# Two low halves by negative and added transfer, one folded sum of squares, and a late scaling of a third unit in a two-layer decoder trunk

## The chip, the cores and the metric

One Trainium2 chip, one core. The metric is the device time of one execution in microseconds, the median of repeated runs. All inputs and outputs are float32.

## The reference

`x` has 256 positions of 1024 channels, and two layers run one after the other.

```python
def pool_conv_layer(x, ...):                       # layer 0
    proj = rms_norm(x, norm_g) @ w_in
    a, bv, bg, z = split(proj)                     # 1024, 1024, 1024, 2048 channels
    ya = (multiscale_pool(a) @ pool_w per group) * pool_scale
    u = causal_depthwise_conv(bv * sigmoid(bg), width 31) + conv_b
    yb = silu(layer_norm(u))
    return (concat(ya, yb) * silu(z)) @ w_out      # added to x

def moba_layer(x, ...):                            # layer 1
    q, k, v, z = split(rms_norm(x, norm_g) @ w_in)
    q, k = rms_norm(q), rms_norm(k)                # by heads of 64 channels
    o = causal_attention(q, k, v) with ALiBi
    return (o * silu(z)) @ w_out                   # added to x
```

## The kernel before, in words

The weights are cut into 49 units of 128 partitions x 2048 columns (1 MB). A unit is one strip of 256 output channels, or 256 rows of an output projection. Names of units (lines 40 to 54): BG and BV (0 to 7), A (8 to 11), ZB (12 to 15), PW (16, the pooling maps), ZA (17 to 20, the gate of ya), OA (21 to 24, the output projection of ya), OB (25 to 28, that of yb), Z1 (29 to 32, layer 1's gate), six pairs of units for k, q and v (33 to 44), O1 (45 to 48).

Most products are made of three matmuls in a faster number format, `product` at line 1074: a float32 operand is split in a high half, rounded by a copy, and a low half, the rest. TensorE takes high x high, high x low and low x high. Five units (`NATIVE`) are multiplied in plain float32 instead; such a matmul appears as two records of the trace.

Each unit comes by a DMA of SyncE into one of four raw slots (L399); the load of unit n waits until unit n - 4 is no longer read. ScalarE copies each half of the unit to its high half (`cut_hi`, L461), which also waits for a free slot of high halves. For the low half there are two ways. VectorE subtracts, `cut_lo`, L740. Or, for the units of `ADDED` (10, 21, 22, 24), ScalarE writes the high half's negative (L464), and a transfer that POOL issues (`added_low`, L426) adds the raw half to it in memory; TensorE then waits for that transfer (`arrived`, line 1081).

The same split is made of the activations. For the output projection of ya, four pairs of tiles are multiplied by their gate on VectorE (L906), copied to `ya_hi` by ScalarE (`high_ya`, L519) and subtracted to `ya_lo` by VectorE (`low_ya`, L887). The pairs belong to units 21 to 24; unit 23 is native and needs no halves. The first two are subtracted after the taps of step 19, and units 21 and 22 wait for them at line 1209.

Every engine's order is written out by hand, step by step (`for n in range(1, OA[0] + 1)` at line 531 for ScalarE, at line 890 for VectorE). A planner (`conv_plan`, line 193) spreads the 31 taps of the depthwise convolution over the steps: some are single operations on VectorE (L856), some are two products on ScalarE (L548) and one addition of two tiles on VectorE (L860), and 28 of them are summed by transfers that POOL issues (L435), joined at L853. The planner counts a unit as 5.75 us (line 202), a native one as 6.9. When the taps are done, VectorE folds the channels' sum (`fold_mean`, L873), TensorE makes the mean of it in the midst of unit 23 (`channel_mean`, L1200), VectorE centres (L880), ScalarE squares (L469), VectorE folds (`fold`, L767), and TensorE makes the variance in the midst of unit 24 (`SUM2_AT`, L1154).

Layer 1 begins while layer 0's residual is still being added: VectorE adds pair by pair (L961), ScalarE squares (L469) and copies the high halves of the unnormalised h to `ya_hi` (L487), VectorE subtracts (`low_h`, L753). Units 29 and 30 (`EARLY`, line 243) are multiplied with these unnormalised halves. The norm's factor comes later: the squares are summed over channels by four matmuls of `square_sums` (L1154, lines 1257 to 1260), ScalarE takes the root (L473), VectorE the reciprocal (L773), and both units' results are multiplied by it out of PSUM on VectorE (`scale_late`, L793) and gated by ScalarE in place (`late_gate`, L492). Units 31 and 32 take the normalised h (`over_rms`, line 781), and ScalarE gates them out of PSUM itself (L675).

The end of that stage is ordered so. ScalarE: late gate 29, late gate 30, cut 33, gate 31, cut 34, gate 32 (lines 667 to 676). VectorE: late scaling 29, late scaling 30, low halves of 33, low halves of 34 (lines 1028 to 1032). From unit 33 on TensorE takes units in pairs, with the activations as stationary operand and 256 columns of each of the two units as one moving operand of 512 (`token_step`, line 1117): its first step waits for the first half of both.

## Time and profile before

| | us |
|---|---|
| median of 3 runs | 329.39 (329.38 to 329.5) |
| the profiled execution, its own time | 329.37 |
| its span, first to last instruction | 327.4 |
| TensorE busy | 321.8 (98%) |
| VectorE busy | 261.1 (80%) |
| ScalarE busy | 235.8 (72%) |
| GpSimd busy | 51.2 (16%) |

Mean granted clock of TensorE: 0.999 of full speed. Engines in rows: PE is TensorE's matmuls, DVE VectorE, ACT ScalarE, POOL GpSimd, SPq the queue of SyncE. L12 is line 12 of the kernel. In a timeline row the first number is the start in us from the start of the span, the second the time from the first start to the last end of the instructions that are merged in the row (their count stands behind x); a bracket gives the idle time of the engine ahead of it, and whose end it waited for. Instructions that follow each other on one engine overlap by about a tenth of a microsecond, so a row of four of 0.69 lasts less than 2.76.

### The profile page before, as it was taken

What the parts mean: (1) busy time and instruction counts of PE and PEld (TensorE: products, weight loads), DVE (VectorE), ACT (ScalarE), POOL (GpSimd) and SP (SyncE); (2) the same over time, 40 slices, a digit from 0 to 9 for tenths busy, and PEclk for the clock granted to TensorE, in tenths of its full rate; (3) what the DMA queues carried; (4) which work ended last, traced back from release to release, by engine and by line L of the source; (5) the groups of instructions that cost most, each with busy time, mean ns of one, the idle gap of its engine ahead of it and who ended that gap; (6) DMA issues with size and microseconds to landing.
All of it is one profiled execution on the core that took longest, in us unless ns stands there. A gap on an engine that the chain in (4) does not pass through costs nothing.

```text
span 327.4 us, 5849 instructions
## 1 busy us (share of the span) xinstructions
PE 321.8 (98%) x2244; PEld 295.5 (90%) x2244; DVE 261.1 (80%) x482; ACT 235.8 (72%) x436; POOL 51.2 (16%) x58
## 2 busy tenths in 40 slices
PE   8999999999999999998999999999999999999995
PEld 8899999999999999997999999988887777778885
DVE  2799989999999999999895898846556887758533
ACT  4687999997999889987766557814756667566630
POOL 0050024423224112120000000005500231400000
PEclk9999999999999999999999999999999999999999
DMA  7988478969999699984539244780635323200003
GB/s 275 413 278 355 156 265 224 203 148 344 346 328 214 122 411 292 217 270 93 249 143 397 104 148 152 279 322 13 243 130 166 132 103 129 114 2 0 2 0 130
DMA packets 12843, 64.79 MB, mean 198 GB/s; under 512 B 1424, under 2 KB 1552, under 8 KB 6544
## 3 DMA queue, kind: packets, MB, share of 16 engines
q1 hardware_dynamic: 8064, 53.78, 43.3%
q0 software_dynamic: 4608, 10.49, 17.7%
q8 instruction: 18, 0.29, 0.4%
q10 hardware_dynamic: 144, 0.15, 0.2%
q14 instruction: 9, 0.07, 0.1%
HBM read 52.88 MB, written 1.05 MB: 165 GB/s over the span
## 4 chain that ended last, share of the span: by engine, by line
PE 90%; ACT 4%; DVE 3%; issue 1%; POOL 0%; DVEq 0%; ACTq 0%; POOLq 0%
PE bank L1077 24%; PE bank L1078 23%; PE bank L1079 23%; PE bank L1111 4%; PE bank L1137 3%; PE bank L1185 2%; PE bank L1291 2%; PE bank L1318 2%; PE bank L1154 2%; PE bank L1145 2%; PE bank L1304 2%; ACT scratch L548 1%; DVE scratch L856 1%; ACT w_hi L461 1%; PE bank L1270 1%
## 5 line engine op out<-in xcount | busy, mean ns | idle before, releaser
L740 DVE TENSOR_TENSOR w_lo<-raw,w_hi 128x1024 fp32r<-128x1024 f32 x80 | 95.3, 1222 | 16.9 <-ACT w_hi L461 16.7
L461 ACT CAST w_hi<-raw 128x1024 fp32r<-128x1024 f32 x88 | 88.6, 1047 | 7.5 <-DMA raw<-w 3.8
L1077 PE MATMUL bank<-h_hi,w_hi 128*128 128x256 f32 x320 | 91.1, 285 | 0.0
L1079 PE MATMUL bank<-h_hi,w_lo 128*128 128x256 f32 x320 | 90.5, 283 | 0.0
L1078 PE MATMUL bank<-h_lo,w_hi 128*128 128x256 f32 x320 | 90.5, 283 | 0.0
L1078 PEld LDWEIGHTS bank<-h_lo,w_hi 128*128 128x128 f32 x320 | 61.4, 192 | 0.1
L1077 PEld LDWEIGHTS bank<-h_hi,w_hi 128*128 128x128 f32 x320 | 61.4, 192 | 0.1
L1079 PEld LDWEIGHTS bank<-h_hi,w_lo 128*128 128x128 f32 x320 | 61.4, 192 | 0.0
L856 DVE SCALAR_TENSOR_TENSOR scratch<-scratch,params 128x256 f32<-128x256 f32 x106 | 43.4, 482 | 0.2
L1077 PE MATMUL bank<-ya_hi,w_hi 128*128 128x256 f32 x144 | 42.6, 296 | 0.0
L1078 PE MATMUL bank<-ya_lo,w_hi 128*128 128x256 f32 x144 | 40.7, 282 | 0.0
L1079 PE MATMUL bank<-ya_hi,w_lo 128*128 128x256 f32 x144 | 40.7, 282 | 0.0
L1077 PE MATMUL bank<-w_hi,h_hi 128*128 128x512 f32 x96 | 39.2, 408 | 0.0
L1078 PE MATMUL bank<-w_lo,h_hi 128*128 128x512 f32 x96 | 37.6, 391 | 0.0
L1079 PE MATMUL bank<-w_hi,h_lo 128*128 128x512 f32 x96 | 37.5, 391 | 0.0
L548 ACT ACTIVATE scratch<-scratch,params 128x256 f32<-128x256 f32 x78 | 32.8, 504 | 0.0
L435 POOL DMA_DIRECT2D side_v<-side_ring x24 | 21.0, 905 | 73.9 <-ACT side_ring L528 52.8
L1077 PEld LDWEIGHTS bank<-ya_hi,w_hi 128*128 128x128 f32 x144 | 27.5, 191 | 2.0 <-issue 1.7
L1078 PEld LDWEIGHTS bank<-ya_lo,w_hi 128*128 128x128 f32 x144 | 27.5, 191 | 0.1
L1079 PEld LDWEIGHTS bank<-ya_hi,w_lo 128*128 128x128 f32 x144 | 27.5, 191 | 0.0
L860 DVE TENSOR_TENSOR scratch<-scratch 128x512 f32<-128x512 f32 x39 | 26.1, 690 | 1.0
L446 POOL TENSOR_SCALAR scratch<-scratch 128x8 f32<-128x8 f32 x8 | 5.1, 632 | 116.5 <-DVE scratch L1037 116.2
(106 smaller groups left out, 522.2 us busy)
## 6 DMA issues: line engine op xcount, KB each, us to landing
raw<-w SPq DMA_DIRECT2D x49, 1024.0 KB, 6.9
side_v<-side_ring POOLq DMA_DIRECT2D x24, 256.0 KB, 6.5
w_lo<-raw POOLq DMA_DIRECT2D x8, 512.0 KB, 7.3
X<-xT SPq DMA_DIRECT2D x2, 512.0 KB, 5.2
out<-X SPq DMA_DIRECT2D x4, 256.0 KB, 2.6
consts<-const SPq DMA_DIRECT2D x1, 290.0 KB, 13.3
params<-vec ACTq DMA_DIRECT2D x1, 149.0 KB, 4.9
```

The source lines that it names most:

```text
L435: pool.dma_start(side_v[:, pair, item % 2, :, :], side_home(pair, item), accum_op=ALU.add).then_inc(side_added[pair][item % 2], 16)
L461: nc.scalar.copy(halves(w_hi, cut_slot(n), half), halves(raw, n % RAW, half)).then_inc(hi_cut, 1)
L548: last = nc.scalar.mul(product_home(product)[:, i, :], U[:, c, k:k + S], column(CW + TAPS * c + k))
L740: nc.vector.tensor_tensor(halves(w_lo, cut_slot(n), half), halves(raw, n % RAW, half), halves(w_hi, cut_slot(n), half).bitcast(F32), ALU.s ...
L856: nc.vector.scalar_tensor_tensor(V[:, c, :], U[:, c, k:k + S], column(CW + TAPS * c + k), V[:, c, :], ALU.mult, ALU.add).then_inc(tap, 1)
L860: nc.vector.tensor_tensor(V[:, c:c + 2, :], V[:, c:c + 2, :], product_home(product), ALU.add).then_inc(tap, 1)
L1077: nc.tensor.matmul(dst, wh, ah, start=start, stop=False, skip_group_check=True)
L1078: nc.tensor.matmul(dst, wh, al, start=False, stop=False, skip_group_check=True)
L1079: return nc.tensor.matmul(dst, wl, ah, start=False, stop=stop, skip_group_check=True)
L1111: last = nc.tensor.matmul(dst, wr, (H if n else H0)[:, k, :], start=start, stop=stop, skip_group_check=True)
L1137: return nc.tensor.matmul(dst, wr, SZ[:, (KD if n in OB else 0) + tile, :], start=start and m % 2 == 0, stop=stop, skip_group_check=True)
L1145: nc.tensor.matmul(bank[7][:, 0:P], ones[:, :], ones[:, :], start=True, stop=True, skip_group_check=True)
```

## The change

Three parts. (A) The low halves of the first two gated pairs of ya are made as `ADDED` units are: after its copy ScalarE writes the negative into `ya_lo`, and a transfer of 256 KB that POOL issues adds the gated tiles. POOL's list is written out, with these two transfers between those of units 21 and 22; the copy and the negative of the second pair stand between the two halves of unit 22 on ScalarE; TensorE waits for the two transfers at units 21 and 22. VectorE's two subtractions are gone. (B) Layer 1's squares are folded on VectorE to one tile, by two more operations at step m = 4, and one matmul behind the sixth step of unit 29 takes the place of four matmuls behind its second and third. (C) Unit 31 joins the units that are multiplied with the unnormalised halves; VectorE scales it and ScalarE gates it in place. Unit 32 is then the first to wait for the normalised halves.

```diff
--- before.py
+++ after.py
@@ -123,6 +123,8 @@
     return sum(1 for n in units[:i] if n not in NATIVE)
 
 
+
+SQUARE_FOLDS = (0, 2, 2, 2), (0, 4, 2, 3), (0, 6, 2, 4), (0, 1, 1, 4)
 
 STEPS = 48
 CUT_HI_AT, CUT_LO_AT = (1, 7, 9, 15), (2, 8, 11, 15)
@@ -239,8 +241,9 @@
 
 
 MEAN_AT = 2, 0, 5
+SUM3_AT = 5
 SUM2_AT = 3, 0, 2
-EARLY = (BG[0],), (Z1[0], Z1[1])
+EARLY = (BG[0],), (Z1[0], Z1[1], Z1[2])
 
 
 def hybrid_trunk(nc, xT, w, vec, const, out):
@@ -331,7 +334,8 @@
         raw_in = [sem(f"raw_in{i}") for i in range(RAW)]
         ones_set, pads_set, qs_set = sem("ones_set"), sem("pads_set"), sem("qs_set")
         hi_cut, lo_cut = sem("hi_cut"), sem("lo_cut")
-        minus_hi = sem("minus_hi")
+        minus_hi, minus_ya = sem("minus_hi"), sem("minus_ya")
+        ya_added = [sem(f"ya_added{i}") for i in range(2)]
         lo_added = [[sem(f"lo_added{n}{half}") for half in range(2)] for n in ADDED]
         unit_done = sem("unit_done")
         sq_ready, folded = sem("sq_ready"), sem("folded")
@@ -418,10 +422,10 @@
                                     ALU.mult).then_inc(qs_set, 1)
             pool.wait_ge(pads_set, 3)
 
-            def added_low(n):
+            def added_low(n, parts=(0, 1)):
 
                 i = ADDED.index(n)
-                for half in range(2):
+                for half in parts:
                     pool.wait_ge(minus_hi, 2 * i + half + 1)
                     pool.dma_start(halves(w_lo, cut_slot(n), half).bitcast(F32), halves(raw, n % RAW, half),
                                    accum_op=ALU.add).then_inc(lo_added[i][half], 16)
@@ -437,9 +441,20 @@
                 if n + 3 in EARLY_ADDED:
                     added_low(n + 3)
 
-            for n in ADDED:
-                if n not in EARLY_ADDED:
-                    added_low(n)
+            def added_ya(i):
+
+                pool.wait_ge(minus_ya, i + 1)
+                pool.dma_start(ya_lo[:, 2 * i:2 * i + 2, :].bitcast(F32), SZ[:, 2 * i:2 * i + 2, :],
+                               accum_op=ALU.add).then_inc(ya_added[i], 16)
+
+            added_low(OA[0], (0,))
+            added_ya(0)
+            added_low(OA[0], (1,))
+            added_low(OA[1], (0,))
+            added_ya(1)
+            added_low(OA[1], (1,))
+            added_low(OA[3])
+
 
             for r in range(8):
                 pool.wait_ge(qk_ss, r + 1)
@@ -517,6 +532,10 @@
                 act.wait_ge(ya_ready, i + 1)
                 act.wait_ge(tap, max(FOLDED[2 * (i // 2):2 * (i // 2) + 2]))
                 nc.scalar.copy(ya_hi[:, 2 * i:2 * i + 2, :], SZ[:, 2 * i:2 * i + 2, :]).then_inc(yahi_ready, 1)
+                if i < 2:
+                    act.wait_ge(yahi_ready, i + 1)
+                    nc.scalar.mul(ya_lo[:, 2 * i:2 * i + 2, :], ya_hi[:, 2 * i:2 * i + 2, :].bitcast(F32),
+                                  -1.0).then_inc(minus_ya, 1)
 
             def side_product(pair, item):
 
@@ -535,8 +554,6 @@
                     cut_hi(OA[3], (0,))
                 if n == ZA[0]:
                     act.wait_ge(tap, PRODUCT_USED[LATE_FROM - 1])
-                if n == OA[0] - 2:
-                    high_ya(1)
                 for tiles, k, product, _, _ in CONV_PLAN.get(n, ()):
                     if product is None or k is None:
                         continue
@@ -549,7 +566,10 @@
                                              column(CW + TAPS * c + k))
                     last.then_inc(product_ready, 1)
                 if n + 3 in (OA[0], SPARE):
-                    cut_hi(n + 3, (0,) if n == ZA[1] else (0, 1))
+                    cut_hi(n + 3, (0,))
+                if n + 3 == SPARE:
+                    high_ya(1)
+                    cut_hi(SPARE, (1,))
                 if n == OA[0]:
                     cut_hi(OA[3], (1,))
                     high_ya(3)
@@ -755,14 +775,12 @@
 
             folds = 0
 
-            def fold(group, pairs):
+            def fold(group, first, last):
 
                 nonlocal folds
-                steps = ((0, 2, 2), (0, 4, 2), (0, 6, 2), (0, 1, 1)) if pairs == 4 else ((0, 2, 2), (0, 4, 2))
-                for i, (a, b, n) in enumerate(steps):
-                    if i < 3:
-                        dve.wait_ge(sq_ready, 4 * group + i + 2)
-                    if i:
+                for a, b, n, squares in SQUARE_FOLDS[first:last]:
+                    dve.wait_ge(sq_ready, 4 * group + squares)
+                    if first or (a, b) != SQUARE_FOLDS[first][:2]:
                         dve.wait_ge(folded, folds)
                     nc.vector.tensor_tensor(SQ[:, a:a + n, :], SQ[:, a:a + n, :], SQ[:, b:b + n, :],
                                             ALU.add).then_inc(folded, 1)
@@ -910,11 +928,11 @@
                     cut_lo(n + 2)
                 if n == OA[0]:
                     fold_mean()
-                for i in {ZA[2]: (0, 1), OA[0]: (3,)}.get(n, ()):
-                    low_ya(i)
+                if n == OA[0]:
+                    low_ya(3)
 
             centre()
-            fold(1, 4)
+            fold(1, 0, 4)
             cut_lo(OB[1], (0,))
             take_inverse(2)
             dve.wait_ge(sq_ready, 8)
@@ -967,10 +985,12 @@
                     residual(m, 0)
                     dve.wait_ge(x_updated, m + 1)
                     gained(1, m)
+                if m == 4:
+                    fold(2, 2, 4)
                 if m:
                     low_h(1, m - 1)
                 if m == 2:
-                    fold(2, 3)
+                    fold(2, 0, 2)
             cut_lo(Z1[1])
             take_inverse(3)
             cut_lo(Z1[2])
@@ -1206,7 +1226,7 @@
                 if n in NATIVE:
                     pe.wait_ge(ya_ready, i + 1)
                 else:
-                    pe.wait_ge(yalo_ready, pairs_cut(OA, i + 1))
+                    pe.wait_ge(*((ya_added[i], 16) if i < 2 else (yalo_ready, 1)))
                 for kt in range(2):
                     arrived(n, kt)
                     for m in range(KD):
@@ -1253,11 +1273,9 @@
                 if n % 4 == 0:
                     pe.wait_ge(root_ready, 3)
                 for k in range(KD):
-                    channel_step(n, k, {Z1[0]: 1, Z1[2]: 2}.get(n))
-                    if n == Z1[0] and k == 1:
-                        square_sums(6, (0, 1), bank[0], False)
-                    if n == Z1[0] and k == 2:
-                        square_sums(0, (6, 7), bank[0], True)
+                    channel_step(n, k, {Z1[0]: 1, Z1[3]: 2}.get(n))
+                    if n == Z1[0] and k == SUM3_AT:
+                        square_sums(8, (0,), bank[0], True)
 
             def turn_qk(octet, isq, half):
 
```

## Rows read from the trace of the kernel before

**Rows 1.** The page's first part: busy time, share of the span, instructions
```profile
PE 321.8 (98%) x2244; PEld 295.5 (90%) x2244; DVE 261.1 (80%) x482; ACT 235.8 (72%) x436; POOL 51.2 (16%) x58
```

**Rows 2.** The waits of TensorE: who for whom, us, times, longest
```profile
PE bank L1200 <- DVE scratch L873: 0.8, 1, 0.8
```

**Rows 3.** Timeline of TensorE: the start, and the two sums of layer 0
```profile
0.98 5.36 PE L1145 MATMUL bank<-ones 128*128 128x128 f32 x24 [0.98 <-POOL eps L411]
...
145.60 2.75 PE L1137 MATMUL bank<-scratch,raw 128*128 128x256 f32 x12
149.21 0.67 PE L1200 MATMUL bank<-scratch,ones 128*128 128x256 f32 x2 [0.84 <-DVE scratch L873]
...
155.10 0.70 PE L1154 MATMUL bank<-scratch,ones 128*128 128x256 f32 x2
```

**Rows 4.** Timeline of VectorE, 118 to 160 us
```profile
131.96 1.29 DVE L887 TENSOR_TENSOR ya_lo<-scratch,ya_hi 128x512 fp32r<-128x512 f32 x2
...
133.96 4.69 DVE L860 TENSOR_TENSOR scratch<-scratch 128x512 f32<-128x512 f32 x6
...
146.65 2.41 DVE L873 TENSOR_TENSOR scratch<-scratch 128x1024 f32<-128x1024 f32 x3 [0.23 <-DVE scratch L860]
...
152.31 2.74 DVE L767 TENSOR_TENSOR scratch<-scratch 128x512 f32<-128x512 f32 x4
```

**Rows 5.** Timeline of ScalarE, 118 to 160 us
```profile
122.82 1.05 ACT L461 CAST w_hi<-raw 128x1024 fp32r<-128x1024 f32 x1 [1.10 <-PE bank L1079]
123.90 1.07 ACT L464 ACTIVATE w_lo<-w_hi 128x1024 fp32r<-128x1024 f32 x1
...
125.35 0.61 ACT L519 CAST ya_hi<-scratch 128x512 fp32r<-128x512 f32 x1
...
132.96 4.90 ACT L548 ACTIVATE scratch<-scratch,params 128x256 f32<-128x256 f32 x12
...
148.74 1.99 ACT L461 CAST w_hi<-raw 128x1024 fp32r<-128x1024 f32 x2 [2.63 <-issue]
150.64 2.42 ACT L469 ACTIVATE scratch<-scratch 128x512 f32<-128x512 f32 x4
```

**Rows 6.** Timelines of GpSimd and of SyncE's queue: two issues
```profile
125.26 0.86 POOL L426 DMA_DIRECT2D w_lo<-raw  x1 [4.76 <-ACT w_lo L464]
...
141.37 0.33 SPq L399 DMA_DIRECT2D raw<-w  x1
```

**Rows 7.** Transfers: issue at 125.26, queue over 134:136, issue at 141.37; KB, us to landing
```profile
w_lo<-raw POOLq DMA_DIRECT2D x1, 512.0 KB, 7.6
...
q0 software_dynamic: 121, 0.43, 108.8%
...
raw<-w SPq DMA_DIRECT2D x1, 1024.0 KB, 7.3
```

**Rows 8.** Timeline of TensorE in layer 1: first sum, first pair
```profile
185.93 1.02 PE L1154 MATMUL bank<-scratch,ones 128*128 128x256 f32 x4
...
209.22 0.40 PE L1077 MATMUL bank<-w_hi,h_hi 128*128 128x512 f32 x1
```

**Rows 9.** Timeline of VectorE, 184 to 209.5 us
```profile
186.31 1.47 DVE L753 TENSOR_TENSOR ya_lo<-H,ya_hi 128x512 fp32r<-128x512 f32 x2
188.03 2.36 DVE L740 TENSOR_TENSOR w_lo<-raw,w_hi 128x1024 fp32r<-128x1024 f32 x2 [0.25 <-ACT w_hi L461]
...
202.16 1.28 DVE L793 TENSOR_TENSOR scratch<-bank,rinv 128x512 f32<-128x512 f32 x2
205.07 4.74 DVE L740 TENSOR_TENSOR w_lo<-raw,w_hi 128x1024 fp32r<-128x1024 f32 x4 [1.64 <-ACT w_hi L461]
```

**Rows 10.** Timeline of ScalarE, 184 to 212 us
```profile
202.87 1.23 ACT L492 ACTIVATE scratch<-scratch 128x512 f32<-128x512 f32 x2 [0.78 <-DVE scratch L793]
204.01 1.98 ACT L461 CAST w_hi<-raw 128x1024 fp32r<-128x1024 f32 x2
```

**Rows 11.** One stretch: busy time by engine, granted clock, DMA share, GB/s
```profile
145.00:150.00 5.00, 4.16 (x23) 3.44 (x22) 4.45 (x8) 2.37 (x4) 0.86 (x1) 1.00 1.04 276
```

## The prediction, made before the changed kernel was run

> **What bounds the kernel now.** I read the engine totals, the waits of TensorE, then the timelines of the three places that the change touches. TensorE is busy 98% of the span [rows 1], so only two things shorten this kernel: less work on TensorE, or fewer of its waits. After the start it waits once, for VectorE's mean fold (L873) [rows 2]. The cover of everything else is thin in places, and a step that grows on ScalarE or VectorE can reach TensorE. So each step is followed to the next TensorE instruction that needs it.
>
> **The mean's wait.** Six native products of unit 23 are twelve records from 145.60 at 0.216 us, so TensorE is ready at 148.2; the fold ends at 149.07 (146.65 + 2.41) and the mean's matmul starts at 149.21 [rows 3, 4]: 1.0 us lost. What sets 149.07? VectorE runs back to back from 138.6. Before that its six product adds take 4.69 us for six operations of 0.69 that elsewhere follow each other every 0.62: it gets each product just as ScalarE finishes the pair (2 x 0.40 us, six pairs from 132.96 to 137.86) [rows 4, 5]. ScalarE itself is busy without a pause from 122.82, when TensorE frees a weight slot, to those products [rows 5]. So the mean hangs on ScalarE's total work between 122.8 and 132.96, not on VectorE's.
>
> **Part A, the low halves of two gated pairs.** Removed: two VectorE subtractions, 1.29 us together at 131.96 [rows 4]. Behind them VectorE waits for ScalarE anyway, so this gives nothing: the time becomes a wait. Added: two negatives of 512 columns on ScalarE. The trace has a negative of 1024 columns (1.07) beside a copy of 1024 (1.05) and a copy of 512 (0.61) [rows 5]. So one of 512 takes about 0.62; it starts 0.03 after its own copy instead of overlapping it by 0.10, and in the queue it costs 0.64. Bounds: 0.5 (the pace of copies that overlap) and 0.75. Both lie ahead of the first product; the move of the second pair's copy behind the first half of unit 22 changes no total. The products, the six adds, the rest of the taps and the fold all move by 2 x 0.64 = 1.28 us: the fold ends at 150.35 and the mean's matmul starts at 150.5. **Term: +1.28** (1.0 to 1.5).
>
> The transfers. POOL now issues five in place of four ahead of unit 22's second half, and that one's negative ends 1.28 later. The first half of unit 21 is issued at 125.26 and lands 7.6 us later, at 132.9 [rows 6, 7]; the second half of unit 22 landed by 141.3, when SyncE issues the load that waits for it [rows 6]. Three more transfers of 512 KB in 8.4 us is close to what the queue moves: 0.43 MB in 2 us, at a 109% share of the engines with hardly another beside it [rows 7]. So 256 KB more is 1.2 us, and behind two of them 2.5. Unit 21 starts two slots of 5.75 us (line 202) ahead of 145.60, at 134.1; its pair lands at 132.9 + 1.2 = 134.1, on the edge. The second pair lands near 140.5, where unit 22 wants it at 139.85, and unit 22's second half near 143.8 where it is wanted at 142.7: together some 1.2 us of waits. They cost nothing by themselves: TensorE would otherwise reach the mean at 148.2 and wait until 150.5, which swallows up to 2.3 us. Anything beyond is lost. VectorE's and TensorE's later steps don't hurry the queue.
>
> What is late next: the load behind it. SyncE issues unit 26's load when unit 22 is done with, at 141.37 now, and it takes 7.3 us [rows 6, 7]; ScalarE cuts unit 26 from 148.74 for 1.99, and only then squares, from 150.64 to 153.06 [rows 5]. 2.5 us later the squares end at 155.55. The fold's last two steps, 0.69 and 0.42 [rows 4], then end at 156.8. TensorE wants that sum at 155.10 + 1.28 = 156.4 [rows 3]. **Term: +0.5** (0, if the transfers cost nothing, to 2, if they cost 4 us).
>
> In a sentence of its own: the Trainium skill (DMA: Bandwidth & Descriptors, Anatomy of one DMA, the GpSimd path) fits such a transfer as 2.0 us plus its bytes over 436 GB/s, which is an estimate of 2.6 us for 256 KB. By it no low half would be late, and the sum would be 0.5 us lower. The trace doesn't agree: 7.6 us for 512 KB where the fit has 3.2 [rows 7].
>
> **Part B, one folded sum.** Removed: three of the four matmuls of layer 1's sum of squares. Two of them are four records, and they push the products behind them by 0.86 (0.216 each, the pace above) [rows 8]; three are **-1.30 us**, all on TensorE's path. Added: on VectorE a fold of 512 and one of 256 columns between two low halves of h, 0.69 + 0.42 by the durations of [rows 4]. From 186.31 the order is low half (0.62), fold, fold, low half: the last ends at 188.65 instead of 187.78, and the subtraction that began at 188.03 (after waiting 0.25 for ScalarE) begins at 188.54 [rows 9]: everything behind it is **0.5 later**. TensorE's fifth and seventh step of unit 29 want the low halves at 187.4 and 189.2 (two and four steps of 0.72, and the one matmul, behind 185.93 [rows 8]); they are there at 187.0 and 188.65. The sum runs at 188.8, 0.9 us later than its last matmul now, the root is ready at 190.0, and VectorE comes to the reciprocal only behind unit 30's two subtractions (2.36), at 190.8: hidden.
>
> **Part C, unit 31 scaled late.** Units 33 and 34 are multiplied as a pair, and the first step of 33 waits for the first low half of 34. Now: ScalarE cuts 33 at 204.01 to 205.99, gates 31 out of PSUM, cuts 34; VectorE subtracts the four halves from 205.07 to 209.81 [rows 9, 10]. The third ends at 208.7, and TensorE starts the pair at 209.22 [rows 8]: 0.55 us of cover. After the change ScalarE must wait for VectorE's scaling of 31 before it cuts 34, and that scaling stands behind both subtractions of 33. With T the start of ScalarE's cut of 33: the low halves of 33 end at T + 3.42; the scaling (1.28 for two, 0.64 at their pace) at T + 4.0; the gate (1.23 for two) at T + 4.65; the first cast of 34 (1.05) at T + 5.6; its subtraction (1.22) at T + 6.85 [rows 9, 10]. T is 204.01 + 0.5 = 204.5, since the late gates hang on the same VectorE sequence. So the half is there at 211.4 and the pair can start at 211.5 (0.14 after its release, as at the mean). Without part B's matmuls TensorE would be ready at 209.22 - 1.30 = 207.9. **Term: +3.6** of wait (2.8, if the handovers overlap better and the 0.5 is absorbed, to 4.1), the cut of 34 being what is queued behind the waiting gate. TensorE has no wait after this place to absorb it [rows 2]. What part C frees, the early need of h's low halves at unit 31, had cover before.
>
> **Sum.** +1.28 + 0.5 - 1.30 + 3.6 = +4.1 against the profiled execution's 329.37 us (span 327.4, 2.0 around it), which stands 0.02 below the median of 329.39: 333.5; as the half microsecond at the folds may vanish in part I say 333.3.
>
> **The rivals.**
> One, **faster**: the cover holds. It is one mechanism: VectorE and ScalarE reach T early enough. If the half of 34 is ready before 207.9, part C costs nothing and part B gives 1.30: 328.1; and 327.1 if the mean's wait of 1.0 goes as well, because VectorE has 1.29 less to do. It needs T at 201.0, 3.5 us ahead of my account. Against it: the late gates end at 204.1 now, with VectorE in front of them nearly without pause [rows 9, 10]. For it: nothing in the rows but that the sequence was read from one execution. Chance 0.08.
> Two, **no difference**: part C's wait is under 0.3 and the mean's delay eats part B: 329.4. Chance 0.05.
> Three, **one delay only**: the negatives are covered, or the pair's wait is half of mine: 331.3 to 332.2. Chance 0.10.
> Four, the **transfers** cost 4 us or more, so unit 22 uses up the 2.3 us and the squares are 2 late: 335 to 336.5. Speaking for it, the DMA engines are full in that stretch [rows 7]. Chance 0.10.
> Five, the **clock**: the granted clock stayed at 1.00 (2.4 GHz) through the wait at the mean [rows 11], but no wait of 3.6 us is in this trace. The 24 warm-up matmuls of 128 columns at the start took 5.36 us [rows 3], where half of 0.216 each would make 2.6; a fall to half speed for as long would cost up to 2.7 us more: 334.5 to 336. The Trainium skill (TensorE: Matmul & The Clock Gate, part 1) has it that an idle engine is put back to the lower clock; by that rule the wait at unit 33 would cost twice. Chance 0.07.
> My forecast, both delays and nothing more (332.3 to 334.3), has 0.60.
>
> **Numbers.** A difference under 0.2% (0.66 us) can't be told from none here. Slower takes the forecast and rivals three to five, 0.87; same 0.05; faster 0.08. The range leaves out rivals one and two and the far part of four and five: 331.3 (329.37 + 1.28 + 2.0 less 1.30) to 335.2 (329.37 with 1.5, 1.5, 4.1 and -1.3, the terms near their upper bounds; that takes in a part of rivals four and five).
>
> **What would show it.** The mean's matmul near 150.5 with a wait of 1 to 2.3 us, VectorE's six adds from 135.2; waits of TensorE for w_lo or ya_lo transfers at units 21 and 22; and, above all, a new wait of TensorE of 3 to 4 us at the first matmul of 512 columns, released by VectorE's w_lo, with ScalarE idle some 2 us before it gates unit 31; L1154's records fall from 26 to 20. I am wrong if the pair starts without a wait, or the mean starts before 149.5.

## The result, and the profile after

The changed kernel takes 337.52 us (median of 4 runs, 337.28 to 338.48) against 329.44: a ratio of 1.0247, 95% interval 1.0228 to 1.0265. It is slower, as forecast, by 8.1 us and not by 3.9; 333.3 was named, and the range ended at 335.2. The profiled execution has a span of 336.7 us, and was itself the slowest of the four, 338.48.

The waits of TensorE in the changed kernel (who for whom, us in total, times, longest):

```profile
PE bank L1097 <- DVE w_lo L760: 3.5, 1, 3.5
PE bank L1097 <- DMA w_lo<-raw: 2.6, 1, 2.6
PE bank L1165 <- POOL eps L415: 1.0, 1, 1.0
PE bank L1174 <- DVE scratch L785: 0.9, 1, 0.9
PE bank L1097 <- DMA ya_lo<-scratch: 0.2, 1, 0.2
```

Where there was one wait [rows 2] there are now four, beside the one at the start. The mean's wait is gone. The first row is the forecast's wait at the first pair. The second is TensorE at the second half of unit 22, the fourth the second sum of squares. The timeline of TensorE puts places to them:

```profile
140.71 0.39 PE L1097 MATMUL bank<-ya_hi,w_hi 128*128 128x256 f32 x1 [0.23 <-DMA ya_lo<-scratch]
...
146.43 0.58 PE L1097 MATMUL bank<-ya_hi,w_hi 128*128 128x256 f32 x1 [2.58 <-DMA w_lo<-raw]
...
150.73 2.75 PE L1157 MATMUL bank<-scratch,raw 128*128 128x256 f32 x12
153.32 0.59 PE L1220 MATMUL bank<-scratch,ones 128*128 128x256 f32 x2
...
160.21 0.70 PE L1174 MATMUL bank<-scratch,ones 128*128 128x256 f32 x2 [0.91 <-DVE scratch L785]
...
216.76 0.47 PE L1097 MATMUL bank<-w_hi,h_hi 128*128 128x512 f32 x1 [3.55 <-DVE w_lo L760]
```

Against [rows 3, 8] that is a ledger. The second sum starts at 160.21 for 155.10: +5.1. The first pair starts at 216.76 for 209.22, +7.5, so 2.4 came between the two: the wait of 3.55 and its restart, less part B's 1.30. The span ends at 336.7 for 327.4, +9.3, so 1.8 more came after the pair, where TensorE doesn't wait. The stretches show what that is (us; busy time of the engines; granted clock; DMA share; GB/s):

```profile
144.00:146.00 2.00, 0.00 (x0) 0.00 (x0) 2.00 (x6) 1.97 (x5) 0.00 (x0) 1.00 1.04 217
146.00:149.40 3.40, 2.97 (x14) 2.97 (x15) 3.13 (x6) 1.56 (x2) 0.86 (x1) 0.51 0.62 187
...
217.50:221.30 3.80, 3.80 (x11) 2.95 (x10) 3.78 (x5) 3.07 (x4) 0.00 (x0) 0.55 0.63 209
```

The granted clock is at half (1.2 GHz of 2.4) for some three and a half microseconds behind each of the two long waits. Eleven matmuls of 512 columns are under way in those 3.8 us, where the kernel before has nineteen in as long a stretch behind its pair (210.0 to 213.8). Some 3.4 us at half the clock lose 1.7 us of TensorE's work.

ScalarE's and VectorE's timelines of the changed kernel around the mean and the squares:

```profile
154.26 1.99 ACT L476 CAST w_hi<-raw 128x1024 fp32r<-128x1024 f32 x2 [6.71 <-issue]
156.16 2.18 ACT L484 ACTIVATE scratch<-scratch 128x512 f32<-128x512 f32 x4
```

```profile
135.42 4.70 DVE L878 TENSOR_TENSOR scratch<-scratch 128x512 f32<-128x512 f32 x6 [0.17 <-ACT scratch L565]
...
148.11 2.41 DVE L891 TENSOR_TENSOR scratch<-scratch 128x1024 f32<-128x1024 f32 x3 [0.23 <-DVE scratch L878]
...
157.34 2.81 DVE L785 TENSOR_TENSOR scratch<-scratch 128x512 f32<-128x512 f32 x4 [0.90 <-ACT scratch L484]
```

The six adds and the mean's fold are 1.46 later than in [rows 4], of which 0.15 was there before (this execution's step at 122.82 is at 122.97): the negatives did what was said. But nobody waited for that fold. ScalarE sat idle 6.7 us until it could cut unit 26, at 154.26 for 148.74 [rows 5]; "issue" is all that the profile names, and the wait in the code is the load of that unit. The squares stand behind the cut, the fold behind the squares, and TensorE behind the fold. The half that the load waits for, by its issue on GpSimd and its landing (KB, us):

```profile
134.33 0.86 POOL L430 DMA_DIRECT2D w_lo<-raw  x1 [1.16 <-ACT w_lo L479]
...
w_lo<-raw POOLq DMA_DIRECT2D x1, 512.0 KB, 12.1
```

It landed at 146.4. The forecast said 143.8. SyncE issues the load of unit 26 behind it, 5.1 us later than the 141.37 of [rows 6] (its issue, and its landing as KB, us):

```profile
146.45 0.33 SPq L403 DMA_DIRECT2D raw<-w  x1
...
raw<-w SPq DMA_DIRECT2D x1, 1024.0 KB, 7.7
```

The cut of unit 26 begins as that load lands, at 154.2.

### The profile page after: what moved, and what is told of

It reads as the page before. It is cut to its first block, busy times and chain, and to the rows that moved or that the text cites. A ratio compares the mean times of both kernels' runs of the same rounds, so it can differ in the third digit from the quotient of the medians.

```text
span 336.7 us, 5845 instructions
## 1 busy us (share of the span) xinstructions
PE 324.5 (96%) x2238; PEld 297.2 (88%) x2238; DVE 261.6 (78%) x483; ACT 237.0 (70%) x438; POOL 53.0 (16%) x60
## 4 chain that ended last, share of the span: by engine, by line
PE 79%; DVE 8%; ACT 4%; issue 4%; DMA 4%; POOL 0%; DVEq 0%; ACTq 0%; SPq 0%; POOLq 0%
PE bank L1097 21%; PE bank L1099 20%; PE bank L1098 20%; PE bank L1131 4%; DMA w_lo<-raw 4%; DVE w_lo L760 3%; ACT w_hi L476 3%; PE bank L1157 2%; PE bank L1205 2%; PE bank L1309 2%; PE bank L1336 2%; PE bank L1165 2%; PE bank L1322 2%; DVE scratch L785 1%; PE bank L1174 1%
## 5 line engine op out<-in xcount | busy, mean ns | idle before, releaser
L1097 PE MATMUL bank<-h_hi,w_hi 128*128 128x256 f32 x304 | 86.6, 285 | 0.0
L1098 PE MATMUL bank<-h_lo,w_hi 128*128 128x256 f32 x304 | 86.0, 283 | 0.0
L1099 PE MATMUL bank<-h_hi,w_lo 128*128 128x256 f32 x304 | 86.0, 283 | 0.0
L1097 PE MATMUL bank<-ya_hi,w_hi 128*128 128x256 f32 x160 | 47.9, 300 | 2.9 <-DMA w_lo<-raw 2.6
L1098 PE MATMUL bank<-ya_lo,w_hi 128*128 128x256 f32 x160 | 45.8, 286 | 0.0
L1099 PE MATMUL bank<-ya_hi,w_lo 128*128 128x256 f32 x160 | 45.7, 286 | 0.0
L1097 PEld LDWEIGHTS bank<-ya_hi,w_hi 128*128 128x128 f32 x160 | 31.2, 195 | 5.5 <-DMA w_lo<-raw 2.8
L1098 PEld LDWEIGHTS bank<-ya_lo,w_hi 128*128 128x128 f32 x160 | 31.3, 195 | 0.1
L1099 PEld LDWEIGHTS bank<-ya_hi,w_lo 128*128 128x128 f32 x160 | 31.1, 195 | 0.0
L1097 PEld LDWEIGHTS bank<-w_hi,h_hi 128*128 128x128 f32 x96 | 18.4, 192 | 9.5 <-issue 6.1
```

Source lines behind the costliest of these rows:

```text
L1097: nc.tensor.matmul(dst, wh, ah, start=start, stop=False, skip_group_check=True)
L1098: nc.tensor.matmul(dst, wh, al, start=False, stop=False, skip_group_check=True)
L1099: return nc.tensor.matmul(dst, wl, ah, start=False, stop=stop, skip_group_check=True)
```

## The experiments

**Parts by themselves.** `a_only` is the changed kernel without B and C, `b_only` and `c_only` are the kernel before with that part.

```diff
 a_only, against the changed kernel:
-EARLY = (BG[0],), (Z1[0], Z1[1], Z1[2])
+EARLY = (BG[0],), (Z1[0], Z1[1])
...
-                if m == 4:
-                    fold(2, 2, 4)
...
-                    channel_step(n, k, {Z1[0]: 1, Z1[3]: 2}.get(n))
-                    if n == Z1[0] and k == SUM3_AT:
-                        square_sums(8, (0,), bank[0], True)
+                    channel_step(n, k, {Z1[0]: 1, Z1[2]: 2}.get(n))
+                    if n == Z1[0] and k == 1:
+                        square_sums(6, (0, 1), bank[0], False)
+                    if n == Z1[0] and k == 2:
+                        square_sums(0, (6, 7), bank[0], True)
```

> Part A alone on the kernel before (four matmuls for layer 1's sum, unit 31 gated as before). Theory one (the transfers): in the changed kernel the second half of unit 22 landed 12.1 us after its issue, TensorE waited 2.6 us for it, ran at half the granted clock for about 3 us, found the mean's fold long done and waited 0.9 us at the second sum: the mean's matmul came 4.1 us later, the second sum 5.1. All of it belongs to part A, so 334.3 to 334.7 us. Theory two, the forecast as written (ScalarE's two negatives move the mean by 1.3, transfers swallowed, 0.5 at the squares): 331.2. If parts B and C also weigh on this stretch, it is between.

333.96 us (332.10 to 334.41), ratio 1.0120 (1.0090 to 1.0149). The median is near theory one, 0.3 us below its range. The scatter is new: of the 13 runs of the kernel before beside it, 12 lie between 329.23 and 329.80. The profiled execution is the fastest, 332.10: the late half lands after 10.7 us instead of 12.1, TensorE waits 1.6 us at unit 22 and 1.0 us at the second sum, which starts 2.7 us later than before, and the mean clock is 0.999. The other three runs have mean clocks of 0.993 to 0.995.

> Part B alone: two more folds, one matmul for four. Theory one: TensorE has 1.30 us less to do, but VectorE is 0.5 us later in front of the low halves of 33 and 34, whose cover was 0.55: the first low half of 34 would be ready near 209.2 where TensorE wants it at 207.9, so a new wait of 1.3 to 1.5 us at the first matmul of 512 columns eats the gain: 329.2 to 329.7. Theory two (the cover of before holds): 328.1, no wait there.

329.74 us against 329.53, ratio 1.0008 (0.9998 to 1.0019): no difference, theory one. Of the 1.30 us 1.1 come back as two waits, of which I had expected only the second:

```profile
PE bank L1080 <- DVE h_lo L756: 0.6, 1, 0.6
PE bank L1080 <- DVE w_lo L743: 0.5, 1, 0.5
```

The first is unit 31, which wants the normalised halves 1.3 us earlier while they come 0.7 later. Part C is what takes that wait away; the forecast had called what it frees covered, which holds only without B.

> Part C alone: unit 31 scaled late, everything else as before. Theory one (the chain cut 33, low halves of 33, scaling of 31, gate of 31, cut of 34): T stays at 204.0, the first low half of 34 is ready at 210.9, so a wait of 1.8 us at the pair: 331.1 to 331.4, with the granted clock staying at full, since the waits of 0.8 and 0.9 us in both kernels left it there. Theory two (a wait of that length drops the clock too, as 3.5 us did): 333 or more, with slices of granted clock near 0.5 behind the wait. If the chain is not the cause: 329.4.

331.58 us, ratio 1.0058 (1.0043 to 1.0073), +2.05: the chain. The time lies just above theory one's 331.1 to 331.4, the wait is 1.66 us for 1.8. TensorE's timeline, and ScalarE's with the idle time in front of the late gate:

```profile
211.03 0.47 PE L1077 MATMUL bank<-w_hi,h_hi 128*128 128x512 f32 x1 [1.66 <-DVE w_lo L740]
```

```profile
208.06 0.63 ACT L492 ACTIVATE scratch<-scratch 128x512 f32<-128x512 f32 x1 [2.08 <-DVE scratch L793]
208.60 1.98 ACT L461 CAST w_hi<-raw 128x1024 fp32r<-128x1024 f32 x2
```

ScalarE waits 2.1 us for VectorE's scaling, and the cut of 34 waits with it. The four runs agree within 0.1 us, all at a clock of 0.998 or more: this wait did not drop it.

**The first term.** ScalarE's two negatives, without their transfers:

```diff
 neg_only, against the kernel before, in high_ya (and low_ya waits for minus_ya):
+                if i < 2:
+                    act.wait_ge(yahi_ready, i + 1)
+                    nc.scalar.mul(ya_lo[:, 2 * i:2 * i + 2, :], ya_hi[...].bitcast(F32), -1.0).then_inc(minus_ya, 1)
```

> The kernel before with ScalarE's two negatives of the gated pairs and nothing else: no transfer for them, VectorE subtracts as before and overwrites the negatives. It isolates the first term of the forecast. Theory one (the mean hangs on ScalarE): the mean's matmul comes at 150.5 for 149.2, TensorE's wait there grows from 0.8 to 2.1, the time is 330.6 to 330.9. Theory two (VectorE sets the mean, ScalarE's work is covered): 329.5.

330.61 us, ratio 1.0033 (1.0020 to 1.0046), +1.10. The mean's matmul in it:

```profile
150.54 0.67 PE L1206 MATMUL bank<-scratch,ones 128*128 128x256 f32 x2 [2.14 <-DVE scratch L877]
```

It is where the forecast put it (150.5), with the wait grown from 0.84 to 2.14 us. ScalarE, which the engine totals show at 72%, sets the mean.

**What the load of unit 25 does.** It was under way together with the late half.

```diff
 a_hold, against a_only:
+                if n == OB[0]:
+                    sp.wait_ge(lo_added[ADDED.index(SPARE)][1], 16)
                 sp.dma_start(raw[:, n % RAW, :], w[stored_at(n), :, :]).then_inc(raw_in[n % RAW], 16)
```

> Part A alone, and SyncE's load of unit 25 (1 MB) held back until the second half of unit 22 has landed. Theory one, contention: the load of unit 25, issued while that transfer was under way in the changed kernel, shares the engines with it; without it the transfer lands after 8 to 9 us instead of 12.1, TensorE waits under 1 us for it, the clock doesn't fall, and the time is 331.0 to 332.5. Theory two, the POOL queue itself is full (five transfers in a row): it lands after 11 us or more all the same, and the time is that of part A alone within 0.5 us.

337.29 us, ratio 1.0230 (1.0213 to 1.0247), worse than part A by 3.3, and outside both theories. The transfer obeyed theory one: it lands after 8.9 us instead of 10.7 to 12.1, and TensorE no longer waits there. But loads 25 and 26 now go out together, and 26 lands 10.9 us after its issue (KB, us to landing; then the timelines):

```profile
w_lo<-raw POOLq DMA_DIRECT2D x1, 512.0 KB, 8.9
...
raw<-w SPq DMA_DIRECT2D x1, 1024.0 KB, 10.9
```

```profile
150.74 0.67 PE L1220 MATMUL bank<-scratch,ones 128*128 128x256 f32 x2 [1.27 <-DVE scratch L893]
...
154.79 1.99 ACT L478 CAST w_hi<-raw 128x1024 fp32r<-128x1024 f32 x2 [7.14 <-issue]
...
160.73 1.22 PE L1174 MATMUL bank<-scratch,ones 128*128 128x256 f32 x2 [3.93 <-DVE scratch L787]
```

Against the profile of `a_only` the second sum comes 2.9 us later. Another 2.3 us are lost behind it, where the granted clock is at half from 159.5 to 166.

This miss showed the cause: what counts is not TensorE's wait for unit 22 but when unit 26 can be cut. Collected from the profiles:

| kernel | cut of 26 starts | second sum starts | between |
|---|---|---|---|
| before | 148.74 | 155.10 | 6.36 |
| a_only | 151.90 | 157.84 | 5.94 |
| a_one (below) | 152.17 | 158.11 | 5.94 |
| a_fill (below) | 153.97 | 159.91 | 5.94 |
| the changed kernel | 154.26 | 160.21 | 5.95 |
| a_hold | 154.79 | 160.73 | 5.94 |

Two casts, four squares, the last folds: 5.94 us in every kernel that has part A and this order, whatever else differs (`after_fill` and `after_order` below have 5.94 and 5.95). Before, the squares took 2.42 us for 2.18, and TensorE did not wait for the fold: it ended at 155.05 [rows 4], just as TensorE came to the sum in its own order at 155.10. There was no cover.

**Fewer bytes.** Part A for the first pair only.

```diff
 a_one, against a_only:
-                if i < 2:
+                if i < 1:
...
-            added_ya(1)
...
-                if n == OA[0]:
-                    low_ya(3)
+                for i in {ZA[2]: (1,), OA[0]: (3,)}.get(n, ()):
+                    low_ya(i)
...
-                    pe.wait_ge(*((ya_added[i], 16) if i < 2 else (yalo_ready, 1)))
+                    pe.wait_ge(*((ya_added[i], 16) if i < 1 else (yalo_ready, 1 if i == 1 else 2)))
```

> Part A for the first gated pair only: one negative, one transfer of 256 KB; the second pair is subtracted by VectorE. Theory one (the cost of part A is the queue's bytes in front of unit 22's second half, and grows faster than they do, since each wait also drops the clock and delays the load behind): half the bytes leave that half landing near 143.5, TensorE's wait there at 0.5 to 1.2 us, swallowed by the mean's wait, and the mean 0.64 later: 330.2 to 331.0. Theory two (any added transfer costs the same): near part A's 333.96.

333.12 us (331.79 to 333.96), ratio 1.0100 (1.0078 to 1.0123). Theory one's price was wrong by more than 2 us. TensorE doesn't wait at unit 22 at all, the mean's wait is 1.0, and still the second sum waits:

```profile
PE bank L1171 <- DVE scratch L784: 1.8, 1, 1.8
PE bank L1217 <- DVE scratch L890: 1.0, 1, 1.0
```

One transfer of 256 KB is enough to put the load of 26 on the path: it goes out 2.1 us later than before (143.50) and takes 8.6 us instead of 7.3. The second sum is 3.0 us late. This execution is the slowest of the four, and the granted clock fell behind that wait of 1.8 us, which cost another 1.5 us (the time behind the second sum, 173.9 us, against 172.4 in `a_only`). The stretch behind it, with the columns as above:

```profile
159.30:162.30 3.00, 3.00 (x17) 3.00 (x17) 2.57 (x4) 2.21 (x5) 0.00 (x0) 0.53 0.83 350
```

**Is it the clock at unit 22?** Dummy matmuls in TensorE's wait.

```diff
 a_fill, against a_only:
+                    if n == SPARE and kt == 1:
+                        pe.wait_ge(sz_ready, 7)
+                        for _ in range(8):
+                            nc.tensor.matmul(bank[3][:, 0:P], ones[:, :], ones[:, :], start=True, stop=True, ...)
                     arrived(n, kt)
```

> Part A alone, with 8 matmuls of 128 columns of the ones tile ahead of the second half of unit 22 (1.8 us of work nobody reads), where TensorE waited 1.6 to 2.7 us for the transfer. Theory one (the granted clock falls because TensorE idles there, in some executions and not in others): filled, it falls in fewer or none, the times draw together at 332.0 to 332.7 with mean clocks of 0.997 and more. Theory two (the scatter of part A between 332.1 and 334.4 is the transfer's own): the scatter stays, median near 333.9.

334.07 us (332.40 to 336.36), ratio 1.0137 (1.0100 to 1.0175). The clock did stay up in three of four runs (1.000 at 332.40, 334.00 and 334.15; the fourth, 336.36, has 0.995), and nothing was gained. So theory two: a scatter of 1.75 us is there with the clock up throughout. TensorE came to the second sum 11.5 us behind its release at unit 22, against 12.9 in the changed kernel where the clock fell, and waited 2.0 us there instead of 0.9.

**Squares first.**

```diff
 a_sq, against a_only:
             act.wait_ge(ya_ready, 4)
-            cut_hi(OB[1])
             for m in range(4):
                 act.wait_ge(centred, m + 1)
                 square(1, m, V)
+            cut_hi(OB[1])
```

> Part A alone, with ScalarE's squares of the centred tiles ahead of the cut of unit 26 instead of behind it. Theory one (the late load of unit 26 held up the squares and so the second sum): the squares follow the centring, TensorE's wait of 1.0 us at the second sum goes to at most 0.2, 331.2 where the clock stays up and about 333 where it falls at unit 22, median 332.8 against part A's 333.96. Theory two (the sum is late for another reason): the same time as part A alone.

332.56 us (331.92 to 333.83), ratio 1.0093 (1.0063 to 1.0123), near theory one: the wait at the second sum is gone. Now the wait at unit 22 counts, 2.1 us in its profile and followed by half the clock for about 3.5 us, for there is no later wait to swallow either.

**Both steps away.** The order of `a_sq` and the held load of `a_hold` together:

> Part A alone with both remedies: squares ahead of the cut of unit 26, and the load of unit 25 held back until unit 22's second half has landed. Theory one (part A costs the two negatives, 1.1 us by the run with negatives alone, and all the rest comes from two steps: that half's late landing, and the load of 26 behind it that holds up the squares): the half lands within 9.2 us, no wait over 0.6 at unit 22, none at the second sum, time 330.5 to 331.3. Theory two (part A has a cost of another kind): 332 or more. The load of 26 lands later still, so a wait at unit 26 could appear.

330.86 us (median of 10), ratio 1.0040 (1.0027 to 1.0052), mean clock 1.000 in every run. Theory one: part A is down to the negatives' cost, within 0.25 us of `neg_only`, and each of the two steps alone was not enough. Its waits of TensorE:

```profile
PE bank L1220 <- DVE scratch L893: 1.3, 1, 1.3
...
PE bank L1097 <- DMA ya_lo<-scratch: 0.2, 1, 0.2
```

**The clock at the pair.** Dummy matmuls in front of it:

```diff
 after_fill, against the changed kernel:
+                        if n == KU[0] and i == 0:
+                            for _ in range(14):
+                                nc.tensor.matmul(bank[7][:, 0:P], ones[:, :], ones[:, :], start=True, stop=True, ...)
                         if i < 2:
                             pair_banks_free(n, i)
```

> The changed kernel, with 14 matmuls of 128 columns of the ones tile put in front of the first pair of units; their result is read by nobody. They keep TensorE busy for about 3.1 of the 3.5 us that it waits there, and end before the wait does. Theory one (the idle time behind the change drops the granted clock, and that costs 1.9 us at the pair on top of the wait): the clock stays at full behind the pair, 335.3 to 335.8 against 337.5. Theory two (the clock has nothing to do with idling, or costs nothing): 337.3 to 337.7.

336.12 us (334.44 to 337.56), ratio 1.0197 (1.0160 to 1.0234), between the two theories. The medians give 1.4 us, with a scatter of 3 us; within one execution it is cleaner, by the time from the first pair to the end of the span. (The profiled execution is the slowest of the four: its late half landed after 12.3 us, and it comes to the pair 0.7 us later than the changed kernel does.)

```profile
213.82 3.29 PE L1377 MATMUL bank<-ones 128*128 128x128 f32 x28
217.50 0.47 PE L1097 MATMUL bank<-w_hi,h_hi 128*128 128x512 f32 x1 [0.40 <-DVE w_lo L760]
```

```profile
216.00:218.00 2.00, 1.60 (x12) 1.40 (x12) 1.87 (x2) 2.00 (x4) 0.00 (x0) 1.00 0.98 414
218.00:220.00 2.00, 2.00 (x10) 1.63 (x10) 1.98 (x3) 2.00 (x3) 0.00 (x0) 1.00 0.19 41
```

The pair waits as long as ever, only with TensorE at work until 0.4 us before it; the clock stays at 1.00, and 335.8 - 217.50 = 118.3 us follow. In the changed kernel it is 336.7 - 216.76 = 119.9, before 327.4 - 209.22 = 118.2. So the clock's fall costs 1.6 to 1.8 us there, shown by taking only the idling away.

**A better order for part C.**

```diff
 fix_bc: the kernel before with B and C, and
             cut_hi(Z1[3])
+            cut_hi(KU[0])
+            cut_hi(KU[0] + 1)
...
             for i, n in enumerate(Z1):
-                if i > 1:
-                    cut_hi(n + 2)
                 to = SZ1[:, 2 * i:2 * i + 2, :]
...
             for i, n in enumerate(Z1):
-                if i > 1:
-                    cut_lo(n + 2)
+                if i == 2:
+                    cut_lo(KU[0])
+                    cut_lo(KU[0] + 1)
```

> Parts B and C without A, in another order: ScalarE cuts both 33 and 34 right behind 32, ahead of the late gates; VectorE scales 29 and 30, subtracts 33 and 34, and scales 31 last. Theory one (the chain through the scaling of 31 is what part C costs, and only that): the first low half of 34 is ready near 207.4 where TensorE wants it at 207.9, no wait at the pair and none at unit 31, all of part B's 1.30 us is gained: 328.1 to 328.3. Theory two (late scaling costs something else as well): 329.4 or more.

328.06 us (328.05 to 328.71) against 329.51, ratio 0.9959 (0.9944 to 0.9974): faster than both kernels, by what part B promised. The four halves on VectorE follow without a pause, and TensorE finds them at the pair:

```profile
202.85 1.28 DVE L794 TENSOR_TENSOR scratch<-bank,rinv 128x512 f32<-128x512 f32 x2
204.04 4.62 DVE L743 TENSOR_TENSOR w_lo<-raw,w_hi 128x1024 fp32r<-128x1024 f32 x4
208.58 0.68 DVE L794 TENSOR_TENSOR scratch<-bank,rinv 128x512 f32<-128x512 f32 x1
```

`fix2` adds to it MEAN_AT = 2, 0, 7 and SUM2_AT = 3, 0, 5.

> The B and C kernel in the better order (328.06), with the mean's matmul two products later and the second sum three products later in TensorE's order (MEAN_AT = 2, 0, 7; SUM2_AT = 3, 0, 5). Theory one (TensorE's wait of 0.8 to 1.0 us at the mean is an order of TensorE ahead of VectorE's fold, and what follows has 0.5 us or more of cover): the mean's wait goes to under 0.3, 327.1 to 327.6. Theory two (the wait moves to the second sum or to unit 25, since VectorE sets both): 328.0.

328.14 us (327.87 to 328.68), ratio 0.9956 (0.9943 to 0.9968), the same as `fix_bc`: theory two by its time. Of TensorE's waits 0.3 at unit 25 is left in place of 0.8 at the mean; 0.15 us of the rest is a later first sum at the start (6.33 for 6.18). What is left is within the differences between executions of one kernel.

**The changed kernel repaired.** `after_order` is the changed kernel with the order of `fix_bc`, `after_all` has the steps of `a_sq` and `a_hold` too.

> The changed kernel with the order of the faster B and C kernel: 33 and 34 cut right behind 32, 31 scaled and gated last. Theory one (the three costs are separate): the wait and the half clock at the pair are gone, 3.6 + 1.9, and part A's cost stays: 328.06 + 4.4 = 332.5, from 331.0 to 333.5 by whether the clock falls at unit 22. Theory two (part A's lateness also feeds the pair's wait): over 334.

331.95 us (331.39 to 333.48), ratio 1.0074 (1.0048 to 1.0100): 5.6 less than the changed kernel from layer 1's order alone, as theory one has it.

> The changed kernel (A, B and C) with all three remedies: 33 and 34 cut early and 31 scaled last, squares ahead of the cut of 26, the load of 25 held back. Theory one (the costs add up and each is its own): the B and C kernel's 328.06 plus the negatives' 1.1: 329.0 to 329.6, that is, no measurable difference from before. Theory two (they don't add): 330.5 or more.

329.85 us (median of 10, 329.47 to 330.40), ratio 1.0005 (0.9992 to 1.0019). No measurable difference from before, and 0.25 above what was expected in us. The costs add up, near enough.

## Why the prediction was right or wrong

**The mean hangs on ScalarE: right.** +1.28 was forecast, +1.10 measured by itself (`neg_only`), the matmul at 150.54 for 150.5. `a_sq_hold`, where VectorE has its 1.29 us less and only the negatives' cost should be left, came out no faster than `neg_only`, so that saving gave nothing.

**Part B: right.** The 0.5 on VectorE came out at 0.6 (unit 30's subtractions begin at 188.71 in `b_only`, 188.03 before, and 0.07 of that was there ahead of the folds), and 328.06 shows the 1.30 once the cover is there. Its own effect on unit 31 was missed in the forecast; the whole change never meets it, because of part C.

**Part C: right.** +3.6 was forecast; the wait measured 3.55. The same sum gave 1.8 for C alone; the wait measured 1.66 and the time 2.05.

**The step that failed is "The transfers", with "What is late next": the term +0.5 (0 to 2) measured 3.8.** The forecast saw both links and mis-sized them. "Unit 22's second half near 143.8" was the queue's own pace, and that was right: with no load beside it the half lands at 143.3 (`a_hold`). Beside the load of unit 25 it landed at 146.4. That load costs the half 1.8 to 3.4 us of its landing, going by 8.8 to 8.9 us in the three kernels that hold it back and 10.7 to 12.3 in those with two added transfers that don't. The forecast took the load's effect as it was before, where it also ran beside that half (issued at 135.38) and the half took 8.4 us; why it costs more behind the added transfers is open. The load of 26 then started 5.1 us later, not 2.5, and the second sum came 5.1 us later; less the 1.28 that the mean had given already, that is 3.8. The slack in front of the sum was read as 1.3 (the mean's delay), which was right; the load's lateness ran past it microsecond by microsecond. Rival four had this at 335 to 336.5 with a chance of 0.10. The argument that TensorE's wait at unit 22 is swallowed was right in a way that I had not meant: it is swallowed by the second sum's wait, not the mean's. One slip changed nothing in the sum: the forecast has POOL issue "five in place of four" transfers ahead of unit 22's second half. In the code they are five in place of three.

**The second thing that failed is the clock, put at nothing in the sum: rival five at 0.07, and it came.** It was priced at up to 2.7 and costs 1.6 to 1.8 at the pair. Behind unit 22 it cost nothing in the changed kernel, as TensorE still waited 0.91 at the second sum; `a_fill`, which kept the clock up there, gained nothing either. I had treated rivals four and five as alternatives to the forecast. But rival four is the forecast's own term at a higher price, and rival five follows from the wait that the forecast itself contains: a sum with a new wait of 3.6 us should have carried the fall of the clock with it. The Trainium skill's rule (TensorE: Matmul & The Clock Gate, part 1) that an idle engine is put back to the lower clock was borne out by the granted clock of 0.55 behind the pair.

**The sum as measured.** In the profiled execution: +5.1 (A) - 1.30 (B) + 3.7 (C's wait and its restart) + 1.8 (clock) = +9.3; the medians have +8.1, since this execution was the slowest of four. Why the late half's landing varies, from 10.7 to 12.3 us over the profiles, was not tried apart.

## What to carry to other kernels

Follow a transfer past the engine that waits for it, to the load that reuses its buffer: here the load of 26, with no cover at all, cost 3.8 us beyond the mean's delay, more than the 2.6 us that TensorE waited for the transfer itself. Before an operation is moved from VectorE to ScalarE, look which of the two the next common result waits for; a busy share of 72% said nothing. And put whatever has its data in hand (the squares, the cut of 34) ahead of what waits for a load or for another engine in an in-order queue.

## What the runs showed of the hardware

The granted clock stayed at full through waits of TensorE of 1.7 us (`c_only`, mean clock 0.998 or more in four runs) and 2.1 (`neg_only`, 0.997 or more in five), and in the profiles of `a_fill` and `after_order` through 2.0 and 2.35. It fell to half behind 1.8 (`a_one`), 2.1 (`a_sq`), 2.6 and 3.5 (the changed kernel), 2.7 (`after_fill`, at unit 22) and 3.9 (`a_hold`). So waits of about 2 us lie on either side, and length alone does not decide it. The longest that left it alone, and the granted clock behind it:

```profile
146.08 0.39 PE L1098 MATMUL bank<-ya_hi,w_hi 128*128 128x256 f32 x1 [2.35 <-DMA w_lo<-raw]
...
146.00:150.00 4.00, 3.92 (x29) 3.81 (x30) 3.70 (x6) 1.38 (x2) 0.86 (x1) 1.00 0.74 230
```

Dummy matmuls of 128 columns kept the clock up in the profile of `after_fill` at the pair, and at unit 22 in three of the four runs of `a_fill`.

Two loads of 1 MB that go out together beside a transfer of POOL's queue took 6.8 and 10.9 us to land in `a_hold`. The load of 26 alone, behind the same wait for the late half, took 6.5 to 8.6 in the others. POOL's queue also has its own pace. With no load beside it, the 512 KB of unit 22's second half landed 8.8 to 8.9 us after their issue behind two added transfers of 256 KB; the four transfers of 512 KB for units 21 and 22 in the kernel before took 7.0 to 8.4, with loads beside the first and the last.
